# Second block: sums of squares of four rows one behind the other in four column strips, rotations of two rows in one product

## The reference

```python
    q = apply_axial_rope(rms_norm_2(p[..., O_Q:O_K].reshape(B, L, N_DIFF_HEADS, 2, DIFF_HEAD_DIM), q_norm_w), rope_tables)
    k = apply_axial_rope(rms_norm_2(p[..., O_K:O_V].reshape(B, L, N_DIFF_HEADS, 2, DIFF_HEAD_DIM), k_norm_w), rope_tables)
```

## Time and profile before

| | |
|---|---|
| time, median of 3 runs | 4021.47 us (4018.49 to 4024.07) |
| span of the profiled execution | 4015.0 us |
| TensorE busy | 3828.8 us, 95% |
| VectorE busy | 2501.9 us, 62% |
| ScalarE busy | 1733.1 us, 43% |
| HBM over the span | 164 GB/s |
| TensorE's share of the chain that ended last | 84% |
| sums of squares, line 1481 | 64 records, 592 to 617 ns |
| rotations, line 1478 | 64 records, 377 to 483 ns |

### The profile page before, as it was taken

One profiled execution on the slowest core, in us unless ns is written; L12 is line 12 of the kernel. 1 busy time (PEld: TensorE's weight loads), 2 busy tenths in 40 slices (PEclk: granted clock), 3 DMA queues, 4 the chain that ended last, 5 costly groups with the idle time before them and its releaser, 6 DMA issues.

```text
span 4015.0 us, 86809 instructions
## 1 busy us (share of the span) xinstructions
PE 3828.8 (95%) x36278; PEld 3255.1 (81%) x36278; DVE 2501.9 (62%) x4423; ACT 1733.1 (43%) x3155; POOL 273.7 (7%) x437
## 2 busy tenths in 40 slices
PE   6999999799989999999999999899999999899999
PEld 2778888566666899989999999878677778787879
DVE  2544588656655687687888888753553553646365
ACT  2544333434333445446454545542343442535344
POOL 0000011232222100000000000000000000000000
PEclk8999999899999999999999999999999999999999
DMA  9422565455555586565667666532222232433335
GB/s 365 154 76 64 187 228 194 161 174 182 186 168 182 193 283 235 188 211 180 225 221 229 223 213 230 200 100 90 65 72 89 64 125 96 139 109 96 120 95 189
DMA packets 289442, 662.43 MB, mean 165 GB/s; under 512 B 21089, under 2 KB 31329, under 8 KB 287537
## 3 DMA queue, kind: packets, MB, share of 16 engines
q1 hardware_dynamic: 233392, 441.74, 33.3%
q0 software_dynamic: 55680, 215.34, 16.6%
HBM read 639.17 MB, written 17.83 MB: 164 GB/s over the span
## 4 chain that ended last, share of the span: by engine, by line
PE 84%; DVE 8%; ACT 3%; issue 2%; DMA 2%; SPq 0%; POOL 0%; DVEq 0%; ACTq 0%; POOLq 0%
PE psum L862 65%; PE psum L827 2%; PE psum L1124 2%; PE psum L1174 1%; DVE wlo L2223 1%; PE psum L887 1%; PE psum L842 1%; DMA ada_head<-in_w_ada 1%; PE psum L1481 1%; ACT whi L1580 1%; DVE smx L2990 1%; PE psum L1189 1%; PE psum L1055 1%; PE psum L965 1%; PE psum L949 1%
## 5 line engine op out<-in xcount | busy, mean ns | idle before, releaser
L2223 DVE TENSOR_TENSOR wlo<-raw,whi 128x512 fp32r<-128x512 f32 (+3 forms) x1568 | 1047.9, 681 | 975.1 <-ACT whi L1580 966.0
L1580 ACT ACTIVATE whi<-raw 128x512 fp32r<-128x512 f32 (+3 forms) x1568 | 971.7, 624 | 1472.7 <-PE psum L862 1450.2
L862 PE MATMUL psum<-hhi,whi 128*128 128x512 f32 (+1 forms) x2416 | 830.6, 344 | 36.9 <-DVE hlo L2263 17.4
L862 PE MATMUL psum<-hlo,whi 128*128 128x512 f32 (+1 forms) x2416 | 811.0, 336 | 0.0
L862 PE MATMUL psum<-hhi,wlo 128*128 128x512 f32 (+1 forms) x2416 | 811.0, 336 | 0.0
L862 PEld LDWEIGHTS psum<-hhi,whi 128*128 128x128 f32 x2416 | 460.6, 191 | 132.4 <-issue 55.9
L862 PEld LDWEIGHTS psum<-hhi,wlo 128*128 128x128 f32 x2416 | 460.6, 191 | 47.6
L862 PEld LDWEIGHTS psum<-hlo,whi 128*128 128x128 f32 x2416 | 461.1, 191 | 46.2 <-issue 2.2
L862 PE MATMUL psum<-fhi,whi 128*128 128x256 f32 x1408 | 400.6, 285 | 6.9 <-issue 4.5
L862 PE MATMUL psum<-flo,whi 128*128 128x256 f32 x1408 | 400.3, 284 | 0.0
L862 PE MATMUL psum<-fhi,wlo 128*128 128x256 f32 x1408 | 400.2, 284 | 0.0
(11 more groups left out here) (440 smaller groups left out, 7031.8 us busy)
## 6 DMA issues: line engine op xcount, KB each, us to landing
raw<-in_w_in SPq DMA_DIRECT2D x328, 512.0 KB, 3.8
ada_raw<-in_w_ada POOLq DMA_DIRECT2D x192, 512.0 KB, 4.6
red_raw<-in_w_adaT POOLq DMA_DIRECT2D x128, 512.0 KB, 4.8
raw<-in_w_out SPq DMA_DIRECT2D x96, 512.0 KB, 3.6
raw<-in_w_gate SPq DMA_DIRECT2D x88, 512.0 KB, 4.9
raw<-in_w_val SPq DMA_DIRECT2D x88, 512.0 KB, 4.2
raw<-in_w_down SPq DMA_DIRECT2D x88, 512.0 KB, 4.7
ada_head<-in_w_ada SPq DMA_DIRECT2D x64, 512.0 KB, 10.2
```

The lines of the kernel that those rows point to most:

```text
L862: mm = pe.matmul(dst, l, r, start=(k == 0 and i == 0 and first), stop=(k == nch - 1 and i == 2), skip_group_check=True)
L1580: act.activation(whi[:, lc % HL, 0:width], raw[:, (lc // 2) % RAW, lc % 2, 0:width], ACT.Copy).then_inc(w_hi, 1)
L2223: dve.tensor_tensor(wlo[:, lc % HL, 0:width], raw[:, (lc // 2) % RAW, lc % 2, 0:width], whi[:, lc % HL, 0:width].bitcast(F32), ALU.subtrac ...
```

## The change

Rotations: rows 2j and 2j+1 are rotated by one product with 512 moving columns (the sequence columns of both rows) into banks 4, 6, 7 and again 4. They stand after k = 4 (j = 0 and 1), 8 (j = 2) and 12 (j = 3). Sums of squares: the four products of rows 0 to 3 stand one behind the other after k = 6, those of rows 4 to 7 after k = 12, behind the last rotation. Each still signals. VectorE reads its half of the doubled bank. The labels and the waits follow: r has four entries, the order in AT_PE is r0, r1, n0 to n3, r2, r3, n4 to n7.

```diff
+            AT_PE[l] += ["r0", "r1"] + [f"n{b}" for b in range(4)] + ["r2", "r3"] + [f"n{b}" for b in range(4, 8)]
             for b in range(8):
-                AT_PE[l] += [f"r{b}", f"n{b}"]
...
-                        for b in {4: (0, 1, 2), 8: (3, 4, 5), 12: (6, 7)}.get(k, ()):
-                            pe.wait_ge(blk_free, b0 + b + 1)
-                            if b >= 3:
-                                pe.wait_ge(at_dve[l], at(AT_DVE[l], f"t{b - 3}", it))
-                            done(pe.matmul(PS[(4, 6, 7)[b % 3]][:, 0:TOK], rotw[:, b // 4, :], qk[:, b, TOK:T2], start=True, stop=True))
-                            pe.wait_ge(at_act[l], at(AT_ACT[l], f"sq{b}", it))
-                            j = 32 * (b % 4)
-                            done(pe.matmul(PS[5][j:j + 32, :], H("sum_k" if b >= 4 else "sum_q"), sq2[:, b % 4, :], start=b < 4, stop=b >= 4,
-                                           tile_position=(0, j), skip_group_check=True))
+                        for j in {4: (0, 1), 8: (2,), 12: (3,)}.get(k, ()):
+                            pe.wait_ge(blk_free, b0 + 2 * j + 2)
+                            if j == 3:
+                                pe.wait_ge(at_dve[l], at(AT_DVE[l], "t1", it))
+                            done(pe.matmul(PS[(4, 6, 7, 4)[j]][:, :], rotw[:, j // 2, :], qk[:, 2 * j:2 * j + 2, TOK:T2], start=True, stop=True))
+                        if k in (6, 12):
+                            half = k // 12
+                            pe.wait_ge(at_act[l], at(AT_ACT[l], f"sq{4 * half + 3}", it))
+                            for j in range(4):
+                                done(pe.matmul(PS[5][32 * j:32 * j + 32, :], H("sum_k" if half else "sum_q"), sq2[:, j, :], start=half == 0, stop=half == 1,
+                                               tile_position=(0, 32 * j), skip_group_check=True))
...
-                            dve.wait_ge(at_pe[l], at(AT_PE[l], f"r{b}", it))
+                            dve.wait_ge(at_pe[l], at(AT_PE[l], f"r{b // 2}", it))
...
-                            own.then(TT(rope2[:, 1, :], PS[(4, 6, 7)[b % 3]][:, 0:TOK], sin, ALU.mult))
+                            own.then(TT(rope2[:, 1, :], PS[(4, 6, 7, 4)[b // 2]][:, b % 2 * TOK:b % 2 * TOK + TOK], sin, ALU.mult))
```

## The result

The changed kernel takes 4000.3 us (median of 14 runs) beside 4023.3 us of the kernel before in the same comparison: ratio 0.9945, 95% interval 0.9936 to 0.9953. That is 22 us less (19 to 26). One of the 14 runs of the changed kernel took 5295.5 us at a mean granted clock of 0.65 and is left out of the ratio. The forecast was 27.5 us less. The direction and the mechanism held; the size is a quarter too large, and the forecast's ratio of 0.9932 lies just outside the interval. Two more comparisons of the same kernel gave 0.9936 (0.9919 to 0.9954) and 0.9947 (0.9932 to 0.9961).

The account below looks back on a forecast made before the run. TensorE was taken as the bound. Interruptions per call of heads fall from 12.87 to 5.98 us (3.44 rotations, 2 x 1.27 sums), 6.89 less, times 4 = 27.5 us: median 4021.47 to 3994.0, range 3988 to 4005.

Parts of the forecast that it names:

- What bounds the kernel: At the edited places VectorE, ScalarE and the weight stream wait for TensorE, which is busy for 95% of the span.
- Merged rotations at nothing: Per call of heads, four rotations of 512 columns cost 3.44 us, the same as eight of 256.
- A fixed cost on top of each product: About 60 cycles per matmul, 25 ns; eight rotation records fewer would bring 0.2 us per call; left out of the sum.
- Four strips at 1.27 each visit: Four sums together behind k=6 and k=12 cost 1.27 us per visit, lower bound 1.20, taken from row strips with four signals.
- the rule on signals: Trainium skill: increments on every tile serialise at about 26 ns each; three more signals, 79 ns in each of eight visits.
- What may become late: Moving the sums of rows 0 to 3 behind k=6 delays ScalarE's squares and later whi; no cost expected.
- The cover of 3.7 us: Chunk 41 is ready at 11.29, TensorE wants it for k=9 at 14.97, so the wait costs nothing.
- the first rival: No cover: TensorE stands 2.6 us per call at k=9, 10.4 us given back, 4004.4 us; chance 0.06.
- the third: ScalarE's stop empties the weight buffers: 7.7 us idle per call at k=9 plus 1.7 for half clock; 4031.6 us; chance 0.02.
- The second: Strips of the sums run one behind the other: a visit costs 3.84 us, total 4014.5 us; chance 0.04.
- The sum against the median: 27.5 us off the whole span, 4015.0 to 3987.5; the median stays 6.5 us above it, at 3994.0.
- the forecast's own range of 3989 to 4000: Range around 3994.0 us for the whole kernel, from two visit prices (0.6 us) and 5.6 us run scatter; forecast's chance 0.86.

Follow-up runs that it names:

- The kernel with the sums alone: Against the changed kernel, rotations go back to one row per product behind k=4, 8 and 12, sums stay as changed; ratio 0.9942 to the kernel before.

## Why the prediction was right, and where it was off

**What bounds the kernel.** TensorE was the bound at every edited place, as the clock of 1.00 and the 70.00 us of 70 said. In the changed kernel it is still without idle time there.

**Merged rotations at nothing.** Right, but with less ground than it seems: the prediction took a rotation of 256 columns as half of 0.86 and then read from the equal totals that there is no fixed cost on top, while no row of before priced such a product by itself. The kernel with the sums alone supplied the price. Three products of 256 columns cost 1.30, so 0.43 each, two of 512 cost 1.73, and all interruptions are 23.4 us in both kernels. A fixed cost on top of each product, which would have brought 0.2 us per call, does not show.

**Four strips at 1.27 each visit.** The term was mis-sized by 0.07: it measured 1.20, the value of the earlier trace rows, not of the earlier trace rows. The step that failed is the choice of the neighbour with four signals, and the sentence that the difference of 0.07 us says the same as the rule on signals. The run with one signal showed that the signals cost nothing here and that row strips are dearer than column strips. With it the sum reads 28.0 us for the interruptions instead of 27.5.

**What may become late.** The cover of 3.7 us was 3.4, the wait cost nothing, and moving the sums two chunks on brought nearly the stall that the account of ScalarE's queue gave (2.59 for 2.7). So the first rival was a real mechanism that stood two chunks away. Of the third, the slow clock showed behind that stall in three calls of four, and the wait for a load from memory in none. The second fell: a visit of four sums reads 1.20 and not 3.84.

**The sum against the median.** This is where the forecast missed. It took for granted that time saved where TensorE is the bound arrives in full at the end. 28.0 us were saved, the comparisons say 22, 26 and 21. 2.7 us of the gap show in three traces of each kernel, behind the idle stretch ahead of the last output projection, where the clock falls in the changed kernel and not in before. That gives 25.3 us, ratio 0.9937, which the intervals of all three comparisons hold. The rest, 0 to 6 us, stays open. The only place where the traces leave room for it is ahead of the first edited place, whose start differs by 6 us between the means of three traces each and by 5 and 10 us within one kernel. The third rival had the half clock in it, but only behind a stall that the change would make; that an old and unchanged idle stretch could turn slow was in none of the cases.

**What was luck.** The measured 4000.3 us lies just outside the forecast's own range of 3989 to 4000. It is inside the stated 3988 to 4005 because that was widened for the first rival, a stall at k=9 that did not come.

## What to carry to other kernels

Small fp32 products into narrow column strips belong next to each other, one for each strip: here one cost 1.18 us and four cost 1.20. Merging plain products of 256 columns into fewer of 512 did nothing. Before moving such a group away from the place where its operands were freed, add up the queue of the engine that waits for it; two chunks here were the difference between no cost and 2.6 us a time, and a slow clock behind it in three calls of four. And a saving of half a per cent should be counted in the trace at the edited places first, because the granted clock behind unchanged idle stretches elsewhere moved the total by 1.4 to 2.7 us at a time, and the start of the edited part scattered by 5 to 10 us.

## What the runs showed of the hardware that was not expected

- Four products of 128x32 weights on 512 columns in four column strips cost 1.20 us, a single one 1.18.
- Four row strips cost 1.27 with four signals and 1.28 with one; the signals are not what makes them dearer.
- An idle stretch of 2.9 us is followed by full clock in the three traces of one kernel and by 0.69 to 0.71 of it over 10 us in six traces of kernels that differ from it only earlier in the program; in three further kernels it is 0.83 to 0.85. Products that nobody reads, put into that stretch, brought 1.00 in both kernels that had them.
- Another idle stretch, of 2.45 us, is followed by full clock in the kernel before and the changed one and by 0.66 to 0.68 over 5 us in four variants.
